# Gate and up projections by Strassen's product in a three-pass float32 FFN kernel

## What is computed

```python
D_MODEL = 1024; SEQ = 512; D_FF = 11 * D_MODEL // 4        # 2816 = 22 blocks of 128

def swiglu(h, w_in, w_out):
    gate, up = jnp.split(h @ w_in, 2, axis=-1)
    return (jax.nn.silu(gate) * up) @ w_out

def modulated_sublayer(x, mod, g_pre, g_post, fn, weight):
    shift, scale, gate = mod[:, 0], mod[:, 1], mod[:, 2]
    h = rmsnorm(x, g_pre) * (1.0 + scale) + shift
    y = rmsnorm(fn(h), g_post)
    return x + weight * (1.0 + gate) * y

# per layer i: mod = (silu(c) @ ada_w[i] + ada_b[i]).reshape(B, 9, 1, D)
```

## Time and profile before

| | us |
|---|---|
| time, median of 3 runs | 3120.8 (3117.79 to 3121.87) |
| span of the profiled execution | 3119.5 |
| TensorE busy in it | 2998.4 (96%) |
| VectorE busy | 1690.3 (54%) |
| ScalarE busy | 1169.4 (37%) |
| four gate and up stages | 253.7, 253.9, 248.0, 244.4 |
| four down stages | 126.2, 125.1, 120.9, 120.9 |

### The profile page before, as it was taken

The page is one execution under the profiler, slowest core; times in us unless marked ns, Lnnn a source line. Parts: engine busy times, 40 slices in busy tenths (PEclk is TensorE's granted clock), DMA queues, the critical chain, the costliest instruction groups (busy, mean ns, idle before and its releaser), DMA issues.

```text
span 3119.5 us, 40915 instructions
## 1 busy us (share of the span) xinstructions
PE 2998.4 (96%) x14714; PEld 2485.1 (80%) x14714; DVE 1690.3 (54%) x2741; ACT 1169.4 (37%) x2047; POOL 624.8 (20%) x369
## 2 busy tenths in 40 slices
PE   7999989999999999979999999999999999999999
PEld 7888878888888888757788888787788777877887
DVE  5545567554565334689531113378477533966763
ACT  3223233222232222466432222364444324544442
POOL 1100002010000000100334443313322233042223
PEclk9999999999999999999999999999999999999999
DMA  5655531555535233210222232302211222032113
GB/s 213 197 180 168 173 109 55 189 192 167 172 115 175 95 101 104 66 28 14 68 81 94 95 107 88 122 28 75 95 48 48 87 99 91 19 107 65 48 48 108
DMA packets 88668, 322.52 MB, mean 103 GB/s; under 512 B 10320, under 2 KB 11088, under 8 KB 87888
## 3 DMA queue, kind: packets, MB, share of 16 engines
q1 hardware_dynamic: 65024, 233.65, 23.1%
q0 software_dynamic: 19520, 71.31, 6.7%
q10 hardware_dynamic: 3984, 15.64, 1.5%
HBM read 312.18 MB, written 6.29 MB: 102 GB/s over the span
## 4 chain that ended last, share of the span: by engine, by line
PE 58%; issue 24%; DVE 8%; POOL 6%; DMA 3%; ACT 2%; ACTq 0%; POOLq 0%; SPq 0%; DVEq 0%
PE psum L379 47%; POOL w_lo L360 6%; PE psum L2190 3%; PE psum L1093 2%; PE psum L436 1%; DMA ada_raw<-ada_in 1%; PE psum L1060 1%; DMA raw<-stream_in 1%; PE psum L447 1%; PE psum L743 1%; DVE pt_lo L1158 1%; DVE tb L498 1%; DVE small L1139 1%; DVE h_lo L507 1%; DVE ta L647 1%
## 5 line engine op out<-in xcount | busy, mean ns | idle before, releaser
L360 POOL TENSOR_TENSOR w_lo<-raw,w_hi 128x1024 fp32r<-128x1024 f32 x221 | 536.2, 2434 | 1605.2 <-ACT w_hi L334 1423.4
L379 PE MATMUL psum<-h_hi,w_hi 128*128 128x512 f32 x1824 | 499.8, 400 | 27.8 <-DVE h_lo L507 9.5
L379 PE MATMUL psum<-h_hi,w_lo 128*128 128x512 f32 x1824 | 488.2, 394 | 0.0
L379 PE MATMUL psum<-h_lo,w_hi 128*128 128x512 f32 x1824 | 486.1, 392 | 0.0
L379 PEld LDWEIGHTS psum<-h_hi,w_hi 128*128 128x128 f32 x1824 | 345.0, 190 | 116.6 <-DVE h_lo L507 15.7
L379 PEld LDWEIGHTS psum<-h_hi,w_lo 128*128 128x128 f32 x1824 | 345.8, 190 | 75.2
L379 PEld LDWEIGHTS psum<-h_lo,w_hi 128*128 128x128 f32 x1824 | 343.7, 188 | 75.5
L348 ACT ACTIVATE w_hi<-raw 128x1024 fp32r<-128x1024 f32 x256 | 258.1, 1048 | 162.2 <-DMA raw<-stream_in 161.9
L354 DVE TENSOR_TENSOR w_lo<-raw,w_hi 128x1024 fp32r<-128x1024 f32 x192 | 228.0, 1221 | 110.7 <-ACT w_hi L348 104.4
L334 ACT ACTIVATE w_hi<-raw 128x1024 fp32r<-128x1024 f32 x177 | 185.5, 1052 | 207.1 <-PE psum L379 108.4
L869 ACT ACTIVATE a_hi<-tb 128x512 f32 (+1 forms) x88 | 55.6, 632 | 547.8 <-DVE tb L914 547.8
(11 more groups left out here) (460 smaller groups left out, 4806.0 us busy)
## 6 DMA issues: line engine op xcount, KB each, us to landing
raw<-stream_in SPq DMA_DIRECT2D x433, 512.0 KB, 3.7
ada_raw<-ada_in POOLq DMA_DIRECT2D x128, 512.0 KB, 4.7
ada_first<-ada_in POOLq DMA_DIRECT2D x4, 1024.0 KB, 17.3
ada_first<-ada_in SPq DMA_DIRECT2D x4, 1024.0 KB, 22.2
x_held<-X ACTq DMA_DIRECT2D x2, 2048.0 KB, 6.8
X<-x_held ACTq DMA_DIRECT2D x2, 2048.0 KB, 8.4
X<-xT_in ACTq DMA_DIRECT2D x1, 2048.0 KB, 9.5
out_x<-X SPq DMA_DIRECT2D x8, 256.0 KB, 2.5
```

What stands on the lines that cost most here:

```text
L360: pool.tensor_tensor(w_lo[:, u % RING], raw[:, u % RAW], w_hi[:, u % RING].bitcast(F32), ALU.subtract).then_inc(lo_ready, 1)
L379: mm = pe.matmul(dst, w[wi], m[mi], start=(first and n == 0), stop=(last and n == total - 1), skip_group_check=skip)
```

## The change

Blocks 0 and 1 of each FFN stay as they are. Blocks 2 to 21 are done in ten pairs. For a pair the eight gate and up blocks of weights form a 2 x 2 matrix (gate, up by even chunks, odd chunks of the input features; "a11", "a12", "a21", "a22", one unit of 128 x 1024 each), and `h` a 2 x 2 matrix (even, odd chunks by first, second half of the tokens). Strassen's product in Winograd's form takes seven products for eight: each is 24 matmuls of 256 columns (`product`), 168 for a pair in place of 96 of 512.

- Four sums of weights for each pair on VectorE (`sum_1_dve` to `sum_4_dve`), and seven units for a pair to be split into halves in place of four. Three new buffers `xr` take a21, a22 and a second load of a22; five loads for a pair in place of four.
- Four sums of `h`, `t_sum`, with their halves `t_hi`, `t_lo`, once for each FFN (`combine_dve`), from an unrounded copy `h_full` that ScalarE writes beside `h_hi`.
- Four products' sums are copied out of PSUM by ScalarE (`keep_act`), and VectorE adds them up (`gate_sum_dve`, `up_sum_dve`) before the Silu and the multiply (`products_dve`).
- The halves of `a` are no longer made beside the gate and up stage, but from the last pair on: 11 pieces of 128 x 1024, eight in the last pair and three in the first steps of the down stage. They lie in the places of `h` and `t`.
- The modulation rows are dealt out anew: one in the gate and up stage of "ffn0" and of "ffn1" (one piece in each of eight pairs), and five, five, four in the down stages of "ffn0", "ffn1", "ffn2", two pieces in each step of one unit, with two accumulators in turn.
- Loops are written out. Low halves of "ffn3" move from GpSimd to VectorE.

```diff
+        def pair_pe(pe, L, j):
+            u = own[L, j]
+            of_a, of_b, of_c = pair_banks(j)
+            def product(r, b, moving, first):
+                pe.wait_ge(lo_ready, u + r + 1)
+                for half in range(2):
+                    mm = three_passes(pe, psum[:, b, HALF * half:HALF * half + HALF],
+                                      unit_blocks(u + r, range(4 * half, 4 * half + 4)), moving,
+                                      first=(first and half == 0), skip=True)
+                prod.give(mm, ("u", u + r))
...
+            product(0, of_b, moving_h(0, 0), True)
...
+            product(1, of_c, moving_t(U), True)
+            pe.wait_ge(snap.sem, snap.at((L, j, "p1")))
...
+            product(2, of_b, moving_t(T2), False)
...
+            product(3, of_a, moving_h(1, 0), True)
+            pe.wait_ge(snap.sem, snap.at((L, j, "u2")))
+            product(4, of_b, moving_t(T3), False)
+            product(5, of_c, moving_h(1, 1), False)
+            pe.wait_ge(snap.sem, snap.at((L, j, "u3")))
...
+            product(6, of_b, moving_t(T4), False)
...
+        ADA_GATE = {"ffn0": 2, "ffn1": 8}
+        ADA_DOWN = {"ffn0": range(3, 8), "ffn1": range(9, 14), "ffn2": range(14, 18), "ffn3": ()}
...
+            for k in range(24):
+                i, ks = k // 4, (2 * (k % 4), 2 * (k % 4) + 1)
+                if k:
+                    split_lo(dve, u1 + k + LEAD)
+                if k < 3:
+                    a_lo_dve(dve, L, 8 + k)
...
+                if i < len(mods):
+                    ada_rows(dve, mods[i], (ada_acc, ada_odd)[i % 2], ks)
...
+                if k % 3 == 2:
+                    post_chunk_dve(dve, own_order, L, k // 3, g1, y_ffn)
...
+        def combine_dve(dve, L):
+            even, odd = (h_full[:, side:NC:2] for side in range(2))
+            first, second = slice(0, HALF), slice(HALF, S)
+            dve.wait_ge(full.sem, full.at((L, NC - 1)))
+            combined.give(dve.tensor_tensor(t_sum[:, U], even[:, :, first], even[:, :, second], ALU.subtract), (L, U))
...
-        with_ada = {"ffn0": [(5, 2)], "ffn1": [(5, 9)], "ffn2": [(2, 16), (3, None)], "ffn3": [(5, None)]}
-        down_ada = {"ffn0": 7, "ffn1": 14, "ffn2": None, "ffn3": None}
```

More of the change, by code:

```diff
@@ L250, in kernel_program @@
         FULL = ("ffn0", ("hy", 1))
+        FFNS = ("ffn0", "ffn1", "ffn2", "ffn3")
         def plan_pre(L):
@@ L290, in plan_ffn @@
[L290 to L300 removed]
+            for c in range(NC):
+                full.plan((L, c))
@@ new lines, in ffn_dve, with ffn_sp @@
+            follow(dve, own_order, L, y_ffn)
+        def ffn_sp(sp, L):
+            u = own[L, "u"]
+            for m in range(4):
+                fetch(sp, u + m)
+            for j in range(PAIRS):
+                fetch(sp, (L, j, "a11"))
+                fetch(sp, (L, j, "a12"))
+                if L == "ffn3" and j == 0:
+                    sp.wait_ge(prod.sem, prod.at(("u", u - 1)))
+                fetch(sp, (L, j, "a21"))
+                fetch(sp, (L, j, "a22"))
+                fetch(sp, (L, j, "last"))
+            for k in range(24):
+                fetch(sp, own[L, "down"] + k)
@@ L3131, in ffn_units @@
         gate, up = blocks(w_in[:, :FF]), blocks(w_in[:, FF:])
-        first = units(np.stack([gate, up], 1))
+        first = units(np.stack([gate, up], 1)[:2])
+        pairs = [units(np.concatenate([m[q, half::2], m[q + 1, half::2]]))
+                 for q in range(2, NF, 2) for m in (gate, up) for half in range(2)]
         down = blocks(w_out)
         second = np.concatenate([units(down[n]) for n in range(NC)])
-        return [first, second]
+        return [first, *pairs, second]
     def pool_units():
```

661 lines of the change are left out of this document (431 added, 230 removed).

## The result

The changed kernel takes 3138.0 us (median of 5 runs, 3131.3 to 3140.1), the kernel before 3120.8; the ratio is 1.0046, 95% interval 1.0033 to 1.0060. It is slower, by about 14 us, where 3111 was forecast. Its profiled execution spans 3137.2 us, 17.7 more than before.

The account below looks back on a forecast made before the run. TensorE was taken to bound the FFNs by its distance of matmul starts. Products -89.6, closings -17.0, down stages +74.1, FFN starts +19.5 and half clocks +3 sum to -10, so 3111 us, range 3068 to 3150.

Parts of the forecast that it names:

- - 17.0: Gate and up stages: twelve closings of modulation rows become two, saving 17.0 us.
- Products: Pairs: matmuls of 256 columns at 117.5 ns make a pair 19.74 for 21.98, saving 89.6 us over forty.
- The start of each FFN: Ten VectorE operations before the first product: TensorE waits 4.8, then half clock 1.7, in three FFNs, +19.5 us.
- The down stages: Two modulation pieces a step make steps of 6.7, so TensorE waits for weights' low halves: together +74.1 us.
- the forecast's own walk: Down stage of "ffn0": 8.6 to the first pieces, 18 steps of 6.7, then units to the end, 149.8 us.
- The half clock in the down stages: Half clocks behind TensorE's waits of 1 to 3 in the down stages: 3 us added.
- Rival 2: Down stages: slower modulation transfers, 0.85 more on 50 steps, +42, 3153 us; decides from 0.2 a step; chance 0.22.
- The sign by which the prediction meant to be found wrong: A piece's release-to-use time in the down stages not being 5.4, or TensorE having gaps between products.
- Rival 3: Pairs: VectorE bounds them, its list taking 20.5 a pair, +0.76 x 40 = 30, 3141 us; chance 0.12.
- Rival 4: Down stages: pieces don't bind, stages at TensorE's own 129.4, 129.4, 127.7 save 59 more, 3052 us; chance 0.06.
- Rival 1: Pairs: matmuls of 256 columns at 113.6 ns throughout, a further 26 saved, 3084 us; chance 0.20.
- Rival 5: Pairs: weight loads bound a matmul of 256 columns at 172 ns, +366 against the sum, 3477 us; chance 0.01.

Follow-up runs that it names:

- e8: Changed kernel with only another order of VectorE's work at the start of each FFN, first product's low half earlier: 3126.3 us.
- e12: Changed kernel with weight loads in the first three down stages bringing 128 of 1024 columns, modulation pieces whole, two buffers: 3100.2 us.
- e11: Changed kernel with loads of the down stages' modulation rows bringing 512 of 1024 columns of a piece, two buffers: 3074.0 us.
- e3: Changed kernel with each modulation row of the down stages reading and adding one of its eight pieces, closings kept: 3052.4 us.
- e10: Changed kernel with six unread filler matmuls of 512 columns ahead of units 3 to 20 in the first three down stages: 3151.8 us.
- e4: Changed kernel with two modulation rows in the pairs of each of the first three FFNs, 4, 3 and 3 in their down stages, two buffers: 3062.5 us.
- e1: Changed kernel with five buffers in place of two for the modulation pieces in the down stages, order of work unchanged: 3075.8 us.
- e5: Changed kernel with five buffers for the modulation pieces and the down stages' pieces three steps later: 3060.6 us.
- e9: Changed kernel with e4's row distribution, three down-stage buffers, no piece in steps 0 to 2, and e8's order at FFN starts: 3047.8 us.
- e6: Changed kernel with e4's row distribution, five buffers in the down stages and no piece in their steps 0 to 2: 3063.0 us.

## Why the prediction was wrong

The forecast was 10 less than before, and the profiled executions show 17.7 more. Of the 27.7 between them the down stages are 31.1 (+108.2 for the 74.1 + 3) and the gate and up stages 1.4 (-85.7 for -89.6 - 17.0 + 19.5); the 5.7 less of the hybrid stages, with 0.9 more between the stages, is spread that happened to lie the forecast's way.

**Products: right.** 117.5 ns was taken (the prediction speaks of four runs of such matmuls and lists three); 117.8 is the mean at the full clock over the 1680 matmuls of each FFN, and between products there is no gap. The stages took 224.4, 230.5, 229.6 and 229.8 for 224, 230, 229 and 229. The two closings that stayed and the ten that left are in that.

**The start of each FFN: right.** Waits of 4.4 for 4.8, none in "ffn0", half clock behind each; e8 took 12 to 15 of the 19.5 back by the reason given, ten operations in one line.

**The down stages: the step that failed.** +74.1 was forecast and +108.2 came; "ffn3" at 121.6 is as forecast, so 34.6 are missing in three stages (164.8, 158.6, 156.2 for 149.8, 149.8, 145.5). Along the forecast's own walk:

- from the last product to the first piece: 6.9, 7.0 and 7.2 for 8.6, so -4.7 in the three;
- the steps in between, 18, 18 and 14 of them: 131.4, 127.6 and 100.6, 7.19 a step where the forecast had 6.7: **+24.6**;
- from there to the end: 26.6, 24.0 and 48.4 for 20.6, 20.6 and 43.1: **+14.7**. TensorE waited again for the pieces of the last steps and went through one more stretch at the half clock.

The sentence that was wrong is "After the change each step of the down stage has two pieces, one from each buffer, so a step cannot be shorter than 1.28 + 5.4 = 6.7", taken as what a step takes. It holds neither as a floor nor as a length. Of a chunk's three steps the first two took 6.0 and 6.1 on average, less than the 6.7, and the third, with the chunk's own work, 9.3 (first chunks left out), where the forecast had 7.05. The forecast let the third step's 7.05 of work cover the fetches. But the chunk's work stands behind both pieces: it covers the fetches for the next step, whose pieces then wait for nothing, and not those of its own. In the example the late piece of the middle step was used until 356.01, its buffer's next load landed at 360.07, and the third step took 8.6.

How much is missing is read from the second piece of each step, since VectorE's line goes through each of its uses. In 34 of the 50 steps no chunk's work covers its fetch, and there it was used 5.84 after the release of its buffer on average (4.0 to 8.7), where the forecast took the 5.4 of one load: 34 x 0.44 = 15 more. The average of 5.5, 5.3 and 5.5 over all pieces that VectorE waited for hides this, because the second piece's load is the one that runs beside the first's and the weights'. The other large part, 11.6, is a wait that the forecast's walk doesn't have: VectorE waits 4.2, 4.0 and 3.4 for TensorE's first chunk, behind the hole at the stage's start and its half clock. (The two are 27 together for the +24.6; small terms go the other way.) In e12, with the weights mostly out of the way, the same 34 fetches took 4.94 from release to use, 34 x 0.9 = 31 less, and the 50 steps took 30.8 less, 6.6 each. In e11, at 4.0, the steps took 5.9 to 6.2, and TensorE's own work with the hole of its start was what bound them.

**The half clock in the down stages** was put at 3. TensorE's time beyond waits and e3's floor was 26. Most of it lay beside VectorE's line, which was late anyway; by e10 some 11 reached that line between the first piece and the last. How much of the +24.6 and of the +14.7 at the ends is the half clock's and how much the landings', the runs don't tell more closely; this split is an estimate.

**Rivals.** Rival 2, slower transfers, was right in part and too dear: 15 of its 42 came (0.3 a step, above the 0.2 from which it was said to decide), and 3138 lies between the forecast and its 3153. That its point of decision was so near to the forecast was the sign that the chances were too far on the fast side. The sign by which the prediction meant to be found wrong did not show it: release to use was near 5.4 on average and there were no gaps between products. Rival 3 did not happen (e4). Rival 4 didn't either; e1 (3076) and e5 (3061) come near its 3052 with three tiles of memory that lay idle, and the rows spread (e9) go below it. Rival 1's cadence came up for a hundred us and more in e1 and e10 and for 30 in e6 (below), not in the pairs of the kernel after. Rival 5 is denied, 117.8 / 229 is 0.51.

## What to carry to other kernels

Moving work off the bottleneck engine's busy stage into one with room pays only if its buffers turn over in the time of a step: ask for the buffer that is fetched while two transfers and the weights are under way, and not for the mean, and count waits of paired buffers as the slower of the two. Here three more buffers (e1) were worth 62 us and one or two pieces a step in place of two, with more of them in the pairs (e4), 76, most of the 86 that the gate and up stages had saved. One more buffer was enough where the rows were spread (e9); with two pieces in every one of 20 steps it was not run. Put nothing that can wait ahead of the operands on which TensorE stands at a stage's start, and no short matmuls of one column ahead of a chain of small ones.
